# Hybrid decoder step on one core: the norm's factor behind the router, a new order ahead of the first expert, and a rearranged last expert

## What is computed

```python
h = h + mem_attend(rms_norm(h, norm_mem), ...)
tok = rms_norm(h, norm_ffn)                      # h * rsqrt(mean(h*h) + eps) * gain
logits = tok @ router_w + router_b               # 32 experts
vals, idx = top_k(logits, 4); gates = softmax(vals)
for e in range(32):                              # c: the gate of e for each token, mostly 0
    x = tok @ w_up[e] + b_up[e]
    gate = minimum(x[:, :1024], 7); up = clip(x[:, 1024:], -7, 7)
    acc += c[:, None] * ((gate * sigmoid(1.702 * gate) * (up + 1)) @ w_down[e] + b_down[e])
y = rms_norm(h + acc, norm_final)
```

## Time and profile before

| | |
|---|---|
| median of three runs | 1264.84 us (1263.46 to 1270.69) |
| profiled execution | 1261.45 us, span of its instructions 1259.6 us |
| PE busy | 1173.7 us, 93% |
| DVE, ACT, POOL busy | 391.0, 224.9, 53.0 us |
| DMA | 452.07 MB, mean 359 GB/s |
| granted clock of TensorE, mean | 0.98 of 2.4 GHz |

### The profile page before, as it was taken

The page is one execution under the profiler, slowest core; times in us unless marked ns, Lnnn a source line. Parts: engine busy times, 40 slices in busy tenths (PEclk is TensorE's granted clock), DMA queues, the critical chain, the costliest instruction groups (busy, mean ns, idle before and its releaser), DMA issues.

```text
span 1259.6 us, 15464 instructions
## 1 busy us (share of the span) xinstructions
PE 1173.7 (93%) x6078; PEld 528.7 (42%) x6079; DVE 391.0 (31%) x908; ACT 224.9 (18%) x444; POOL 53.0 (4%) x68
## 2 busy tenths in 40 slices
PE   7997688988899999999999999999999998999997
PEld 5774556776433333333333333333323232333342
DVE  2376970243422232222323222222213121222212
ACT  1245551142211101011111101011111111010112
POOL 2127100000000000000000000000000000000000
PEclk9998799998899999999999999999999999999999
DMA  9234256279599999999999999999999999999993
GB/s 373 87 134 175 94 191 219 76 299 429 201 399 427 428 428 426 427 429 427 430 425 430 426 430 425 428 427 427 427 428 426 428 427 428 428 427 430 424 430 139
DMA packets 44216, 452.07 MB, mean 359 GB/s; under 512 B 5485, under 2 KB 6409, under 8 KB 18024
## 3 DMA queue, kind: packets, MB, share of 16 engines
q1 hardware_dynamic: 41663, 437.06, 82.9%
q0 software_dynamic: 2480, 14.02, 2.9%
HBM read 448.68 MB, written 2.61 MB: 358 GB/s over the span
## 4 chain that ended last, share of the span: by engine, by line
PE 62%; DMA 21%; DVE 13%; ACT 2%; issue 2%; POOL 0%; SPq 0%; DVEq 0%; ACTq 0%
PE psum L1200 20%; DMA mem<-in_w_up_dram 20%; PE psum L1237 15%; PE psum L701 4%; PE psum L1187 3%; PE psum L998 2%; DVE mem L2131 2%; PE psum L1154 2%; PE psum L906 2%; DVE mem L1897 2%; DVE mem L2123 1%; DVE mem L2126 1%; PE psum L1178 1%; ACT mem L1627 1%; DVE mem L2128 1%
## 5 line engine op out<-in xcount | busy, mean ns | idle before, releaser
L1200 PE MATMUL psum<-mem 128*64 128x512 f32 x2048 | 455.7, 595 | 15.6 <-DMA mem<-in_w_up_dram 13.5
L1200 PEld LDWEIGHTS psum<-mem 128*64 128x64 f32 x2048 | 142.5, 137 | 304.0 <-issue 275.3
L1237 PE MATMUL psum<-mem 128*64 128x512 f32 x1024 | 236.9, 600 | 0.0
L1237 PEld LDWEIGHTS psum<-mem 128*64 128x64 f32 x1024 | 66.6, 136 | 133.2 <-issue 112.6
L2123 DVE TENSOR_SCALAR mem<-psum 128x512 f32<-128x512 f32 x32 | 22.1, 692 | 280.5 <-PE psum L1200 280.5
L1627 ACT ACTIVATE mem<-mem 128x512 f32<-128x512 f32 x32 | 20.1, 629 | 471.6 <-DVE mem L2123 471.6
L1364 ACT ACTIVATE mem<-psum 128x512 f32<-128x512 f32 (+5 forms) x137 | 68.0, 546 | 141.4 <-PE psum L701 43.5
L2118 DVE TENSOR_TENSOR mem<-mem,psum 128x528 f32<-128x528 f32 x64 | 45.1, 704 | 131.8 <-PE psum L1187 131.8
L2108 DVE TENSOR_SCALAR mem<-mem 128x64 f32<-128x64 f32 x102 | 25.6, 310 | 128.8 <-PE psum L1172 99.4
L1187 PE MATMUL psum<-mem 128*128 128x264 f32 x256 | 65.5, 398 | 0.0
L1146 PE MATMUL psum<-mem 128*64 128x512 f32 x256 | 61.8, 604 | 1.4 <-DVE mem L2046 1.4
(11 more groups left out here) (327 smaller groups left out, 915.5 us busy)
## 6 DMA issues: line engine op xcount, KB each, us to landing
mem<-in_w_up_dram SPq DMA_DIRECT2D x128, 2048.0 KB, 32.9
mem<-in_w_down_dram SPq DMA_DIRECT2D x64, 2048.0 KB, 34.7
mem<-in_w_in_dram SPq DMA_DIRECT2D x8, 868.0 KB, 14.6
mem<-in_w_o_dram SPq DMA_DIRECT2D x1, 4096.0 KB, 14.2
mem<-in_cache_mem_k_dram SPq DMA_DIRECT2D x1, 4096.0 KB, 14.9
mem<-in_cache_mem_v_dram SPq DMA_DIRECT2D x1, 4096.0 KB, 21.3
mem<-in_w_mk_dram SPq DMA_DIRECT2D x1, 2048.0 KB, 8.2
mem<-in_w_mv_dram SPq DMA_DIRECT2D x1, 2048.0 KB, 14.3
```

What stands on the lines that cost most here:

```text
L1200: ins = pe.matmul(ps[64 * o:64 * o + 64, :], lhs, w[:, k % 2, g * 1024 + o * 512:g * 1024 + (o + 1) * 512], start=False, stop=(k == 7), sk ...
L1237: ins = pe.matmul(pso[64 * o:64 * o + 64, :], lhs, w[:, k % 4, o * 512:(o + 1) * 512], start=(k == 0), stop=(k == 7), skip_group_check=True)
```

## The change

The gain is multiplied into the router's weights, the router works on the plain residual in four quarters of the array (`route`), and a second product with the 0/1 table `fold32` adds the four quarters and turns them to rows; the token's factor is applied with the bias. The square sums come out as one column for each token. ACT makes `h_gain` (residual times gain), which is transposed in place of `xnT`, and applies the factor in its copies. Ahead of the first expert the bias products come first, `n_loops` is computed and loaded early, and the item products go last. The last expert takes its residual by transposes, both halves of the rows before it lie stacked in 128 partitions, and their spread goes behind the up products. The diff is cut to lines that differ, and moved left.

```diff
@@ -184,10 +185,10 @@
     js += [("smv", 0), ("smv", 1), ("omt", 0), ("omt", 1)]
-    js += [("mo", m) for m in range(KD)]
+    js += [("mo", 0), ("mo", 1), ("rq",)] + [("mo", m) for m in range(2, KD)]
...
     js += [("rl",)]
-    js += [("xr", r, g) for r in range(3) for g in range(2)]
+    js += [("xr", r, g) for g in range(2) for r in range(3)]
@@ -366,6 +367,7 @@
 diag = at(temp_off + 864, P)
+rq_s = temp[:, 2, :]
@@ -384,6 +386,9 @@
 xdiag = at(temp_off, 3, P)
...
+h_gain = [at(qT_off + k * NT, NT) for k in range(KD - 1)] + [temp[:, 3, :]]
+std_t, rstd_t = stat[:, 24:27], stat[:, 28:31]
@@ -564,9 +569,7 @@
     load_part(8, 1)
-    for r in range(3):
-        for g in range(2):
-            wait_filled(sp, "xr", r, g)
+    wait_filled(sp, "ss", 3)
@@ -1093,28 +1096,51 @@
     pe.wait_ge(S("w_mo_in"), 16)
+    def route(k):
...
+        wait_drained(pe, "mo", k)
+        return pe.matmul(rq[32 * (k % 4):32 * (k % 4) + 32, 0:NT], rw_sb[:, k, :], hT[:, k, :],
+                         start=(k < 4), stop=(k >= 4), skip_group_check=True)
...
         done(ins, "mo", m)
-    sum_squares(3)
+        if m == 1:
+            rq = take(pe, "rq")
+            pe.wait_ge(S("router_in"), 32)
+        if m == 5:
+            for k in range(4):
+                route(k)
+    for k in range(4, KD):
+        ins = route(k)
+    done(ins, "rq")
+    b = take(pe, "ss", 3)
+    pe.wait_ge(S("squares_added"), 2 * (KD - 2))
+    for r in range(3):
+        pe.matmul(b[0:ROWS[r], r:r + 1], xnT[:, 0, r * P:r * P + ROWS[r]], ones[:, 0:1],
+                  start=(r == 0), stop=False, skip_group_check=True)
+    pe.wait_ge(S("squares"), 2 * KD)
+    for r in range(3):
+        ins = pe.matmul(b[0:ROWS[r], r:r + 1], xnT[:, KD - 1, r * P:r * P + ROWS[r]], ones[:, 0:1],
+                        start=False, stop=True, skip_group_check=True)
+    done(ins, "ss", 3)
     b = take(pe, "rl")
-    pe.wait_ge(S("router_in"), 32)
+    pe.wait_ge(S("late_tables_in"), 16)
+    wait_drained(pe, "rq")
     for r in range(3):
-        for k in range(KD):
-            if r == 0:
-                pe.wait_ge(S("xn_ready"), 2 * KD + k + 1)
-            ins = pe.matmul(b[0:ROWS[r], r * NE:(r + 1) * NE], xnT[:, k, r * P:r * P + ROWS[r]], rw_sb[:, k, :],
-                            start=(k == 0), stop=(k == KD - 1))
+        ins = pe.matmul(b[0:ROWS[r], r * NE:(r + 1) * NE], rq_s[:, r * P:r * P + ROWS[r]], const("fold32"),
+                        start=True, stop=True)
     done(ins, "rl")
-    for r in range(3):
-        for g in range(2):
+    for g in range(2):
+        pe.wait_ge(S("xn_ready"), 2 * KD + 4 * g + 4)
+        for r in range(3):
...
                 k = 4 * g + i
-                ins = pe.transpose(b[0:ROWS[r], i * P:(i + 1) * P], xnT[:, k, r * P:r * P + ROWS[r]], ident)
+                ins = pe.transpose(b[0:ROWS[r], i * P:(i + 1) * P], h_gain[k][:, r * P:r * P + ROWS[r]], ident)
@@ -1146,13 +1172,16 @@
-    def gather_samples_and_bias():
+    def bias_rows():
...
                           start=True, stop=False, skip_group_check=True)
...
+    def gather_samples():
@@ -1258,7 +1287,8 @@
         turn_activations()
-        gather_samples_and_bias()
+        bias_rows()
+        gather_samples()
@@ -1270,18 +1300,20 @@
-    def turn_residual(r, half):
+    def turn_residual(r):
...
         w, ps = ROWS[r], tiles[r][0]
-        for k in range(4 * half, 4 * half + 4):
-            pe.matmul(ps[0:w, k * P:(k + 1) * P], hT[:, k, r * P:r * P + w], ident,
+        for k in range(KD):
+            pe.matmul(ps[0:w, k * P:(k + 1) * P], hT[:, k, r * P:r * P + w], ident, is_transpose=True,
...
-    def spread_before_last(r, half):
+    def spread_before_last(r):
...
         w, ps = ROWS[r], tiles[r][0]
-        pe.matmul(ps[0:w, half * 512:(half + 1) * 512], ST[0:64, r * P:r * P + w],
-                  outb[0:64, half * 512:(half + 1) * 512], start=False, stop=False, skip_group_check=True)
+        for o in range(2):
+            rows = slice(64 * o, 64 * o + 64)
+            pe.matmul(ps[0:w, o * 512:(o + 1) * 512], ST[rows, r * P:r * P + w], outb[rows, 0:512],
+                      start=False, stop=False, skip_group_check=True)
@@ -1299,49 +1331,42 @@
                 turn_slots(gated)
-                for half in range(2):
-                    turn_residual(0, half)
+                turn_residual(0)
             elif part == 1:
-                for half in range(2):
-                    turn_residual(1, half)
+                turn_residual(1)
...
                 turn_slots(gated_l)
-            elif part == 2:
-                pe.wait_ge(S("rows_out"), n + 1)
-                pe.wait_ge(S("rows_out2"), n + 1)
-                for r in range(2):
-                    for half in range(2):
-                        spread_before_last(r, half)
-        pe.wait_ge(S("gate_ready"), n + 1)
-        turn_residual(2, 0)
-        spread_before_last(2, 0)
+        pe.wait_ge(S("rows_out"), n + 1)
+        for r in range(2):
+            spread_before_last(r)
...
         turn_activations()
-        turn_residual(2, 1)
-        spread_before_last(2, 1)
+        turn_residual(2)
+        spread_before_last(2)
...
+    pe.wait_ge(S("expert_bias_in"), 32)
+    pe.wait_ge(S("masks_ready"), 2)
+    bias_rows()
     gather_prompts(1)
-    pe.wait_ge(S("expert_bias_in"), 32)
-    gather_samples_and_bias()
-    pe.wait_ge(S("items_found"), 2)
-    pe.matmul(item_bank[:, 0:LIST], ones, diag_e, start=True, stop=True)
-    pe.matmul(item_bank[:, 128:128 + LIST], ones, diag[:, 0:LIST], start=True, stop=True
-              ).then_inc(S("items_spread"), 1)
-    turn_tokens(1)
+    gather_samples()
+    pe.wait_ge(S("list_ready"), 1)
+    loops = pe.value_load(n_loops[0:1, :], min_val=1, max_val=2)
...
     ins.then_inc(S("gates_turned"), 1)
+    turn_tokens(1)
+    pe.wait_ge(S("items_found"), 2)
+    pe.matmul(item_bank[:, 0:LIST], ones, diag_e, start=True, stop=True)
+    pe.matmul(item_bank[:, 128:128 + LIST], ones, diag[:, 0:LIST], start=True, stop=True
+              ).then_inc(S("items_spread"), 1)
...
     wait_drained(pe, "pos")
-    pe.wait_ge(S("st_copied"), 1)
-    pe.wait_ge(S("list_ready"), 3)
-    loops = pe.value_load(n_loops[0:1, :], min_val=1, max_val=2)
@@ -1371,6 +1396,9 @@
             act.activation(xnT[:, m, :], hT[:, m, :], ACT.Square).then_inc(S("squares"), 1)
+            if n == 3:
+                act.activation(h_gain[m], hT[:, m, :], ACT.Copy, scale=gains[:, 16 + m:17 + m]
+                               ).then_inc(S("xn_ready"), 1)
@@ -1584,13 +1612,20 @@
     squares(3, "mo")
-    root(3)
-    for r in range(3):
+    b = result(act, "ss", 3)
+    act.activation(std_t[:, 0:2], b[:, 0:2], ACT.Sqrt, bias=stat[:, 61:62], scale=1.0 / D)
+    act.activation(std_t[0:TS, 2:3], b[0:TS, 2:3], ACT.Sqrt, bias=stat[0:TS, 61:62], scale=1.0 / D
+                   ).then_inc(drained("ss", 3), 1)
+    wait_filled(act, "xr", 2, 0)
+    act.wait_ge(S("rstd_ready"), 2)
+    for r, g in ((0, 0), (0, 1), (2, 0), (2, 1), (1, 0), (1, 1)):
         w = ROWS[r]
-        for g in range(2):
-            b = result(act, "xr", r, g)
-            out = xn01[:, r, g * 512:(g + 1) * 512] if r < 2 else etab[0:TS, g * 512:(g + 1) * 512]
-            copy(out.rearrange("p (c q) -> p c q", c=4), b[0:w, :].rearrange("p (q c) -> p c q", c=4), "xr", r, g)
+        b = result(act, "xr", r, g)
+        if (r, g) == (1, 0):
+            wait_filled(act, "xr", 2, 1)
+        out = xn01[:, r, g * 512:(g + 1) * 512] if r < 2 else etab[0:TS, g * 512:(g + 1) * 512]
+        act.activation(out.rearrange("p (c q) -> p c q", c=4), b[0:w, :].rearrange("p (q c) -> p c q", c=4),
+                       ACT.Copy, scale=rstd_t[0:w, r:r + 1]).then_inc(drained("xr", r, g), 1)
@@ -1618,7 +1653,7 @@
-    def expert(b, n, pair, last):
+    def expert(b, n, pair, last, own_rows=True):
@@ -1632,7 +1667,7 @@
             turn_out(ST, pair)
-        if not last:
+        if own_rows:
@@ -1640,8 +1675,8 @@
             expert(i % 2, j * BODY + i, j * (BODY // 2) + i // 2, False)
-    expert(0, loops * BODY, loops * (BODY // 2), False)
-    expert(1, loops * BODY + 1, loops * (BODY // 2), True)
+    expert(0, loops * BODY, loops * (BODY // 2), False, own_rows=False)
+    expert(1, loops * BODY + 1, loops * (BODY // 2), True, own_rows=False)
@@ -1995,11 +2030,18 @@
         ins.then_inc(drained("omt", s), 1)
+    dve.wait_ge(S("router_in"), 32)
+    dve.tensor_tensor(rw_sb, rw_sb, gains[:, 16:24].unsqueeze(2).to_broadcast([P, KD, NE]), ALU.mult
+                      ).then_inc(S("dve_step"), step())
...
         add_product(3, "mo", m)
-    for m in range(KD):
-        wait_drained(dve, "mo", m)
-    norm(3, 16)
+    b = result(dve, "rq")
+    dve.tensor_copy(rq_s, b[:, 0:NT]).then_inc(drained("rq"), 1)
+    wait_drained(dve, "ss", 3)
+    dve.reciprocal(rstd_t[:, 0:2], std_t[:, 0:2]).then_inc(S("dve_step"), step())
+    dve.reciprocal(rstd_t[0:TS, 2:3], std_t[0:TS, 2:3]).then_inc(S("rstd_ready"), 1)
```

(26 more changed lines are left out.)

3 lines of the change are left out of this document (2 added, 1 removed).

## The result

| | before | after |
|---|---|---|
| median | 1264.84 us (1262.66 to 1270.69, 5 runs) | 1250.95 us (1249.39 to 1255.58, 5 runs) |
| profiled execution, span | 1261.45, 1259.6 us | 1249.39, 1247.6 us |
| PE, DVE, ACT busy | 1173.7, 391.0, 224.9 us | 1168.1, 386.7, 227.6 us |

After to before is 0.9903, with a 95% interval of 0.9883 to 0.9924: faster by 9.6 to 14.8 us, and by more than the 0.5% that a measurement can tell.

A forecast was written before the change was run, and what follows sets the result against it. The weight stream, restarted once part 0 is read, was taken as the bound. Head 9.2 plus tail 4.4 gave 13.6 us off 1261.45, so 1247.9 profiled and 1251.2 us median; range 1245 to 1259.

The forecast's parts named there:

- head: Work ahead of the expert loop, up to the stream's restart: 10.2 us saved at full clock, 9.2 us after the clock charge.
- tail: Last expert: PE ready 5.6 us earlier, but the last up part waits for its load, so 4.4 us saved.
- What bounds the kernel: Expert loop: weight stream at 424 to 430 GB/s from the twelfth slice; earlier first read of part 0 moves the end equally.
- Router: Ahead of the loop: logits near 307.4 us instead of 315.88, gain 8.5 us, bounds 7.5 and 9.3.
- Gates: Ahead of the loop: ACT's copies and exponentials, done at 314.6 us, hold DVE's gate product; gain 8.6 us instead of 9.4.
- Entry to the loop: From item products to first up product: 0.9 us, middle of 0.4 to 1.4, where it had been 1.4.
- Clock: PE ahead of and into the first expert: possible low granted clock, charged at 1.0 us, chance near one half.
- low clock: Rival: first expert's first part wholly at low clock, 1 to 1.5 us lost, gathers up to 1 more: 1253.5 us; chance 0.26.
- 10.2 us at full clock: Head gain before the clock charge, from a first up product between 320 and 322.7 us, middle 321.4.
- Late bias load: Rival: POOL's expert bias load lands near 324 to 325 us, head gains 3.3 us less: 1254.5 us; chance 0.08.
- Does not do what it says: Rival: accumulating transposes still need two records, register load hides nothing; tail 3.6, head 1 us less: 1253 us; chance 0.10.
- Slower stream: Rival: restarted weight stream takes 60.1 us instead of 58.8 a pair, at fifteen pairs 1270.7 us; chance 0.06.

The follow-up runs named there:

- e11: The changed kernel, unaltered, run again on another chip: median 1250.87 us, ratio 0.9905 to the kernel before.
- e1: The changed kernel with the old last expert, so only the new head: median 1256.40 us, ratio 0.9936 to the kernel before.
- e2: The kernel before with only the new last expert: median 1260.61 us, ratio 0.9963 to the kernel before.
- e4: The changed kernel with the first expert's bias products back behind the gathers: median 1251.50 us, 37.71 us from output products to part 10.
- e9: The changed kernel with the spread of the two prompt blocks back ahead of the last up part: one run at 1253.51 us.
- e7: The changed kernel with the loop count loaded last again, in its old place with its old waits: one run at 1254.41 us.
- e5: The changed kernel with bias products behind the gathers and five filler products only in PE's idle time: median 1250.20 us, ratio 0.9876 to before.
- e3: The changed kernel with unused dense products added on PE in gaps and between steps: median 1251.06 us, ratio 0.9903 to before.
- e8: The changed kernel with the last expert's residual made by products with the identity again: one run at 1251.61 us.
- e12: e5 run again, beside the changed kernel on one chip: median 1248.76 us, ratio 0.9872 to the kernel before.
- e6: The kernel of e3 with four 128x128 transposes in place of each filler product: one run at 1250.69 us.
- e13: The same program as e4, run once more: one run at 1252.19 us, 40.46 us from output products to part 10.

## Why the prediction was right, and where it was not

**Median.** Predicted 1251.2, measured 1250.95. The profiled execution was to take 1247.9 and took 1249.39; the sum was 13.6 us, and the span fell by 12.0. So against the traces the sum was 1.6 us too large: 2.1 us too much in the head, 0.3 us too little in the tail, and 0.2 us that the execution of after gained ahead of both. By the medians the change gave 13.9 us, and 13.8 on another chip (1264.66 and e11's 1250.87); where they get 2 us more than the two profiled executions, no run shows, and both sums lie within the interval of 9.6 to 14.8. That the median came out to 0.25 us is therefore luck, since the terms behind it did not.

**What bounds the kernel.** Right, but for a slice: the stream moves 424 to 430 GB/s from the thirteenth on, the twelfth of the earlier trace rows has 399. The stream begins when part 0 has been read, its pairs take the same time as before, and head and tail move the end by what they are in themselves (e1, e2).

**Router.** Logits predicted at 307.4, measured 307.20. That is 8.7 us ahead of before, but this execution is 0.2 us ahead from the first output product on, so the gain is the 8.5 that were predicted. Last route product predicted at 303.8, measured at 304.0; square sums at 305.2 to 305.8, measured at 305.34. Mask at 310.31 (310.6), slots at 313.88 (313.9).

**Gates.** Wrong for this execution. I had ACT as the last condition of DVE's gate product, at 314.6. Its exponentials ended at 313.14 and the product began at 313.79, where DVE came to it. I had given six copies until 312.5, with transposes at the low clock; the clock held, 24 transposes took 2.84 us instead of the 4.84 of the earlier trace rows, and the copies ended at 311.1. Where the transposes did run at the low clock for the most part, the forecast's wait is there: DVE's gate product waits 0.87 us for ACT's exponentials in e4 and 0.86 in e9. The error cost nothing in the result, since DVE's diagonals, done at 318.00 (predicted 318.7), were waited for by nobody.

**Entry to the loop.** Predicted 0.9 us of what had been 1.4, measured none: the item products end at 322.55 and the first up product starts at 322.58. With the count loaded ahead, PE's instructions for register and branch are done while products are queued (at 316.1 and 320.8). e7 shows the price of the other way, 1.82 us, 0.5 of them for the list. My range from 0.4 to 1.4 left the true value out at its lower end.

**Clock.** This is the term that was mis-sized. What happened is the rival "low clock", with a chance of 0.26: the clock was down from 312.4 to 326. I charged 1.0 us, as half of one event. A second share stood in the sum unnamed: the "10.2 us at full clock" were the middle between a first up product at 320 and one at 322.7, and the later of the two already held the gathers at the low clock. With its early end, 320, and part 10 issued 3.84 us behind it as in the earlier trace rows, the head would be 36.1 us, and e5 measured 36.39 at full clock.
The steps on PE show where the time went. I had the samples' products end at 316.6 to 318.3; they ended at 320.00. The gathers at the low clock I had, but not that bias products at the low clock would hold them up by 0.5 us (slots ready at 313.88, gathers from 314.42), nor the samples' own 1.97 us: bias, gathers and samples took 1.98 + 3.68 + 1.97 us, at full clock 1.09 + 1.94 + 1.07 by e3. The item products so began at 321.60, 1.0 us behind my latest value of 320.6. The first part took another 5.35 - 3.65 = 1.7 us more. What was too high elsewhere hid part of this: the entry by 0.9 us, gates, tokens and items by 0.4. So the head came out only 2.1 us below my 9.2.
Against e5 the low clock costs after about 4.2 us (40.58 - 36.39). That is an estimate: e5 has the other order of the bias, and its fillers still hold the gathers up by 0.5 us. Both executions of after had the low stretch of 13.6 us, and so had e1 and e8; e7, with the same steps up to the entry, had it longer; e9, with after's head too, had the clock low in two stretches and needed 41.18 us. No execution of the new head without fillers read the first part at full clock.
The Trainium skill, "TensorE: Matmul & The Clock Gate", Part 4, says that the full clock doesn't engage for transposes, since they don't count as busy in the same way; the durations that it gives beside this are of bf16. Here, in float32, five stretches speak against it for the rise: the clock came back while transposes alone ran in the kernel before (at 319.5 by the 0.73 of its window in the earlier trace rows, where I had read 319.3), in e2, in e4 (back at 313.6, transposes from 310.1 to 314.6), in e9 and in e12. e6 speaks for it for the fall, with fillers of half the time. What the two have in common isn't settled.

**Late bias load.** Didn't happen. POOL issued it at 308.50 beside parts 8 and 9, and it landed 7.9 us later, at 316.4. The row is in the page's issues (issuer, KB, median us to landing), again:

```profile
mem<-in_b_down_dram POOLq DMA_DIRECT2D x1, 128.0 KB, 7.9
```

**Does not do what it says.** Didn't happen: eight records for a residual block (16 in e8), and a loop count that costs nothing.

**Slower stream.** Pairs of 60.0 us stand at two places of after (984.33 to 1044.30, and the last, 1162.08 to 1222.05), one of them where before has its own. So it isn't new, and nothing accumulates.

**Tail.** 4.4 predicted, 4.7 measured. The last up part was bound by its load as forecast: 1178.3 + 43.7 = 1222.0. From part 10's issue to the start of the last up part it is 893.9 us in after and 898.7 before, from there to the end 25.5 in both. So all of the 4.7 us lie ahead of the last up part, and the 0.3 us beyond the forecast are its landing, 43.7 us after the issue where the earlier trace rows have 44.1. The work behind the activation kept its length, as forecast. The two residual blocks were worth 1.0 us each on PE, as predicted, and what would have brought the start ahead of the landing was lost in the wait.

## What to carry to other kernels

Where a weight stream bounds a kernel, find what starts it and what stands behind its last landing, and cost only these two stretches; as long as PE waits for loads in the loop, time saved there should be worth nothing (argued from the waits, no run changes the loop alone). Once the dependent chain is shortened, the engine that had waited becomes the bound, and its clock is then a term of its own: cost every step of it at both clock levels and give the two sums, since one program can run at either (e4 and e13). A middle taken between bounds must not hide one of the levels. Load a loop's count while work is still queued, since behind the last product the same entry was a stall of 1.8 us.
